# A mixture-of-experts layer on one core: the summing matmuls placed behind each block's gate/up matmuls, the down loads moved forward four blocks later, the halves of b_down side by side

## The reference: what is computed

```python
logits = hf @ w_router + b_router
top_v, top_e = lax.top_k(logits, TOP_K)          # 4 of 32
gates = jax.nn.softmax(top_v, axis=-1)
...
def expert_block(args):                          # for the tokens of one expert
    xblk, e = args
    gu = xblk @ w_gu[e] + b_gu[e]                # 1024 -> 2048
    gate = jnp.minimum(gu[:, :D_FF], SWIGLU_LIMIT)
    up = jnp.clip(gu[:, D_FF:], -SWIGLU_LIMIT, SWIGLU_LIMIT)
    act = (up + 1.0) * gate * jax.nn.sigmoid(SWIGLU_ALPHA * gate)
    return act @ w_dn[e] + b_dn[e]               # 1024 -> 1024
...
return h + moe                                   # sum over a token's experts, weighted by its gates
```

## Time and profile before

| | |
|---|---|
| time, median of 3 runs | 1166.12 us (1165.85 to 1166.32) |
| time of the profiled execution | 1166.64 us |
| its span in the profile | 1164.8 us, that is 1.84 us less |
| PE busy | 1106.0 us, 95% |
| DVE, ACT, POOL busy | 23%, 13%, 1% |
| moved by the DMA queues | 427.28 MB, mean 367 GB/s over the span |

### The profile page before, as it was taken

How to read it: one execution, slowest core, us unless ns; L and a number is a source line. 1 busy time by engine, 2 the same in 40 slices (tenths; PEclk the granted TensorE clock), 3 DMA queues, 4 the chain that set the end, 5 groups by cost and what they waited for, 6 DMA issues and landing times.

```text
span 1164.8 us, 13191 instructions
## 1 busy us (share of the span) xinstructions
PE 1106.0 (95%) x5236; PEld 446.8 (38%) x5236; DVE 269.5 (23%) x621; ACT 151.8 (13%) x285; POOL 8.0 (1%) x28
## 2 busy tenths in 40 slices
PE   9999989999999999989999999999999999999996
PEld 7855755533333333333333333333333333333332
DVE  3643344321111112121111111111111111111111
ACT  3521324400000000000000000000000000000000
POOL 1000000000000000000000000000000000000000
PEclk9999999999999999999999999999999999999999
DMA  9593110999999999999999987999999999999993
GB/s 326 97 383 119 73 73 5 397 416 428 426 429 428 429 429 427 432 430 388 419 432 431 430 362 291 433 429 430 431 430 431 431 430 431 431 430 430 432 428 145
DMA packets 36605, 427.28 MB, mean 367 GB/s; under 512 B 6083, under 2 KB 8228, under 8 KB 17380
## 3 DMA queue, kind: packets, MB, share of 16 engines
q1 hardware_dynamic: 34004, 426.33, 87.7%
q10 hardware_dynamic: 2576, 0.59, 0.2%
HBM read 424.29 MB, written 2.62 MB: 367 GB/s over the span
## 4 chain that ended last, share of the span: by engine, by line
PE 84%; DVE 7%; DMA 5%; issue 3%; ACT 1%; SPq 0%; DVEq 0%; ACTq 0%
PE bank L1629 36%; PE bank L1669 19%; PE bank L1569 5%; PE bank L1250 5%; DMA store<-in_w_down_dram 4%; PE bank L1257 4%; PE bank L1443 3%; PE bank L1617 3%; PE bank L1321 2%; DVE conv L1125 2%; DVE conv L1128 1%; DVE conv L1115 1%; PE bank L1655 1%; PE bank L1372 1%; DMA store<-in_w_in_dram 1%
## 5 line engine op out<-in xcount | busy, mean ns | idle before, releaser
L1629 PE MATMUL bank<-store,conv 128*64 128x512 f32 x2048 | 453.2, 597 | 0.0
L1629 PEld LDWEIGHTS bank<-store,conv 128*64 128x64 f32 x2048 | 142.8, 137 | 305.6 <-issue 304.0
L1669 PE MATMUL bank<-store,conv 128*64 128x512 f32 x1024 | 228.7, 599 | 9.9 <-DVE conv L1128 7.4
L1114 DVE TENSOR_SCALAR conv<-bank 128x512 f32<-128x512 f32 x32 | 22.1, 692 | 694.7 <-PE bank L1629 694.7
L1669 PEld LDWEIGHTS bank<-store,conv 128*64 128x64 f32 x1024 | 71.1, 138 | 144.9 <-issue 127.3
L748 ACT ACTIVATE conv<-conv 128x512 f32<-128x512 f32 x32 | 20.1, 629 | 542.9 <-DVE conv L1114 542.9
L1569 PE MATMUL bank<-qkT 64*128 64x512 f32 x256 | 63.6, 615 | 0.7 <-ACT qkT L755 0.7
L1372 PE MATMUL bank<-arena,qkT 128*64 128x512 f32 x256 | 62.2, 605 | 0.2 <-DVE qkT L927 0.2
L1250 PE MATMUL bank<-store 128*128 128x512 f32 x128 | 57.3, 600 | 0.0
L755 ACT COPY qkT<-bank 128x512 f32<-128x512 f32 x32 | 18.7, 585 | 281.1 <-PE bank L1669 281.1
L1655 PE MATMUL bank<-ident,conv 128*128 128x128 f32 x128 | 21.0, 287 | 24.3 <-DVE conv L1125 24.3
(11 more groups left out here) (284 smaller groups left out, 575.9 us busy)
## 6 DMA issues: line engine op xcount, KB each, us to landing
store<-in_w_gate_up_dram SPq DMA_DIRECT2D x42, 4096.0 KB, 23.5
store<-in_w_down_dram SPq DMA_DIRECT2D x64, 2048.0 KB, 13.8
store<-in_w_gate_up_dram SPq DMA_DIRECT2D x44, 2048.0 KB, 18.6
store<-in_w_in_dram SPq DMA_DIRECT2D x7, 2048.0 KB, 22.3
store<-in_w_out_dram SPq DMA_DIRECT2D x1, 4096.0 KB, 18.8
bias_by_distance<-store SPq DMA_DIRECT2D x1, 1536.0 KB
hx<-in_x_dram SPq DMA_DIRECT2D x2, 512.0 KB, 3.9
store<-bias_by_distance SPq DMA_DIRECT2D x1, 1024.0 KB, 8.3
```

The source lines that it names most:

```text
L1629: ins = mm(dst[SLOTS * hf:SLOTS * (hf + 1), :], xgT[:, c:c + SLOTS], store[:, slot_at(k, odd) + c0:slot_at(k, odd) + c0 + 512], start=Fals ...
L1669: ins = mm(bank[7][SLOTS * hf:SLOTS * (hf + 1), :], actT[:, c:c + SLOTS], w[:, hf * 512:(hf + 1) * 512], start=f == 0, stop=f == KT - 1)
```

## The change

1. `LATE_BLOCKS` goes from 16 to 20: the steps 16 to 19 of SP's loop now issue G(b+1) ahead of D(b), step 20 puts D between the halves, and D goes first from step 21 on (before: from step 17).
2. In the blocks from 10 on, other than the last, `combine()` moves from behind step k = 3 to behind the whole of gate/up, as it stands in blocks 1 to 9.
3. In `add_mixture` the two matmuls with `b_down` stand next to each other, and then the two with `ident`.

```diff
-LATE_BLOCKS = 16
+LATE_BLOCKS = 20
...
                     mm(bank[2 * t + hf][:], gT[t][rows, :], bdn[rows, :], start=False, stop=False,
                        skip_group_check=True)
+                for hf in range(2):
                     mm(bank[2 * t + hf][:], ident[:], hx[:, t, 512 * hf:512 * (hf + 1)], start=False, stop=False,
                        skip_group_check=True)
...
-                    if k == (5 if last else 3) and (whole or last):
+                    if k == 5 and last:
 
                         pe.wait_ge(y_ready, b)
                         combine()
-                        if last:
-                            turn_gates(b)
+                        turn_gates(b)
...
             def whole_block(b, odd):
                 gate_up(b, odd, whole=True)
+                pe.wait_ge(y_ready, b)
+                combine()
                 rest(b)
```

## The result

The changed kernel took 1150.44 us (median of 4 runs, 1148.77 to 1151.44) against 1166.22 us for the kernel before. The ratio is 0.9861, with a 95% interval of 0.9844 to 0.9879. Both lie within 1.2 us of the predicted 1149.5.

What follows compares the result with a forecast made beforehand. PE bounds the kernel before; after the change the loads do: G(30) lands at 1090.8, plus 20.6 to block 31, plus 36.7 gives span 1148.1, profiled 1149.9, predicted 1149.5 us; range 1146.5 to 1154.

Steps and rivals of the forecast that it cites:

- b_down: Between blocks 9 and 10: pairs on different rows and banks run side by side, saving 2.5 us in all.
- the rival: Ahead of G(12): b_down pairs save nothing, 2.0 to 3.4 us idle remain, time 1151.5 to 1153; chance 0.12.
- The turn: Where SP's order puts D ahead of G: queue idle 1.5 us before D(21), in place of 13.1 now.
- The early pockets: Queue idle 2.0 us at G(12)'s first half and 1.4 at its second; both taken as closed by earlier issue.
- Where PE waits: For down in blocks 18 and 19, some 1.5 us each; for gate/up in blocks 27 to 30, some 1.8 each.
- G(30)'s landing and block 31's start: End of the load chain: G(30)'s second half lands at 1090.8, block 31 starts 20.6 us later at 1111.4.
- The end: From block 31's start to the span's end: 36.7 us, taken as untouched by the change.
- What part 1 is worth: LATE_BLOCKS 20: about 4 us, as a turn at step 16 idles 5.1 to 5.6; nothing without part 2.
- PE remains the bound: Whole kernel: no waits for loads, block 31 starts at 1100.6, time 1139; chance 0.03.
- `combine`'s place isn't what PE waits for: Late blocks: the 1.18 us come from something else, only b_down counts, time 1164; chance 0.03.
- such a fall: Blocks 27 to 30: clock falls in PE's 1.8 us load waits, costing 2.7 us once; time 1152 or 1153; chance 0.13.
- The slower case: After the turn, every D(b) meets an empty queue, 3.0 us idle a block, time 1179; chance 0.03.

Runs made afterwards that it cites:

- bdown_only: Only the loop split in add_mixture that pairs the b_down matmuls, against the kernel before: 1163.62 us, ratio 0.9975.
- combine_late20: The full change without the add_mixture loop split (b_down as before): 1152.55 us, ratio 0.9877 to the kernel before.
- clock_fill: The full change plus seven unused 128x256 matmuls where the last block waits for the activation: 1147.64 us, ratio 0.9833 to the kernel before.
- late20_only: Only LATE_BLOCKS = 20, against the kernel before: 1166.14 us, ratio 0.9997.
- half_down: The full change, loading only half the down weights of blocks 9 to 29 (output not the layer's): 1138.85 us, ratio 0.9748 to the kernel before.
- combine_only: Only combine moved behind gate/up from block 10 on, against the kernel before: 1155.64 us, ratio 0.9909.
- last_behind: The full change plus combine and turn_gates behind gate/up in the last block too: 1145.90 us, ratio 0.9822 to the kernel before.
- the two padded kernels: The full change, and last_behind with two unused filling matmuls, each with 4.3 us PE time added between blocks 23 and 24: 1152.75 and 1146.90 us.

## Why the prediction was right

Its steps, against the profile:

- **A block on PE**: 27.5 us forecast, 27.51 measured; both waits on DVE gone.
- **b_down**: 2.5 forecast, 2.5 measured (8.4 to 5.9). Block 10's gate/up started at 520.8, 521.3 forecast. The alternative, that the pair would not run side by side, fell with bdown_only. What it would have cost, the pocket ahead of G(12), is seen in combine_late20, with 1152.55 us in the rival's 1151.5 to 1153.
- **The pace of the loads**: from D(10)'s landing at 533.0 to G(30)'s at 1090.8 it is 557.8 us, less 2.6 lost, over 19 blocks: 29.22 us, 29.26 forecast.
- **The turn**: 1.5 us idle forecast, 1.6 measured; D(21) was issued at 825.0 (824.6 forecast). What it cost before was read too low: ahead of D(16) the prediction counts 2.7 us, but the queue had been empty since G(17)'s first half landed at 692.6, so 3.4 were lost. All in all 17.2 us were lost before, not 15.9 or 16.5. Nothing in the sum hung on it.
- **The early pockets**: the first closed as forecast. The second didn't quite: G(12)'s second half came 0.65 us late and G(13)'s 0.4. In the repeat of the full change neither was late. The second was no pocket in the prediction's sense. Before, from 545.13 to 556.25, the queue had a DMA share of 0.97, and in combine_late20 G(12)'s second half was issued 5.5 us ahead of the first half's landing and still came 1.2 us late. So an earlier issue is not what closes it.
- **Where PE waits**: for down in blocks 18 and 19, forecast with 1.5 us each. Measured were 1.15 and 1.43 (0.27 + 1.16), and already 0.48 in block 17. In blocks 27 to 30 it waits 1.48 us each, 1.8 forecast.
- **G(30)'s landing and block 31's start**: 1090.8 and 1111.4 forecast, 1090.8 and 1111.45 measured. That exactness is luck: D(10) landed 0.4 us earlier than before, the pace took 0.7 less than reckoned, and the queue lost 1.1 more. In the repeat the two are 1089.65 and 1110.34. The weights of the last block were in time, as forecast, but the times given for them, 1110.5 and 1120.3, are those of G(31)'s two halves (1111.6 and 1121.4 measured); D(31) landed at 1131.2.
- **The end**: 36.7 us forecast from there, 38.25 measured. This term was mis-sized. I took it from the earlier trace rows as untouched; the clock falls in the wait of 3.28 us there, and it stayed low for 6.8 us where before it was 3.4. clock_fill shows that the low clock behind that wait is what these microseconds are: with the gap filled, down takes 7.09 us in place of 10.02. Two profiles of the same kernel end 38.25 and 36.7 us after block 31's start, so it varies from run to run; it is 1.5 of the 2.6 us by which these two spans differ.
- **What part 1 is worth**: about 4 us forecast. Block 31's start moved by 2.8 us against the first profile of the full change, and by 3.9 against the repeat, counted from D(10)'s landing; the times, 0.7 to 0.9 us apart, don't settle it. The step that was off is the idle time of a turn at step 16, 5.1 to 5.6 forecast, 4.2 measured: D(17) was issued at 711.0 as reckoned, but G(17) had landed at 709.5 in place of 709.0, and D(17) took 7.6 us, the lower of the two values. That it is worth nothing without part 2 is shown by late20_only.

Of the rivals, "PE remains the bound" has its time, 1139, in half_down, where the loads are fewer; with all loads it isn't so. That `combine`'s place isn't what PE waits for fell with combine_only, 11 us without `b_down`. The clock never fell in a waiting block: it is 1.00 from 828 to 1127, with waits of 1.48 us. The prediction had given such a fall 0.13. The slower case, a queue that goes empty ahead of every D(b), didn't come: one gap only, at the turn.

What the full change leaves is the loads' pace (11.6 us by half_down) and the last block's wait for the activation (4.7 us by last_behind).

## What to carry to other kernels

Where two resources are near their limits, work out both streams as clocks of their own, with the last landing that the rest hangs on, and take the later one; the time saved on the first counts only until the second takes over. Idle time of the slower stream costs one for one, wherever it lies, and nothing while the other is slower: the same shift of the turn moved the last block by nothing where PE was the slower, and by 2.8 us where the loads were. Ask then what triggers each load, since work on the faster engine still counts where it delays an issue, and look at the last round by itself, where a wait has no next round behind it to fill it.

## What the runs showed of the hardware that was not expected

- Second halves of gate/up land late, with the queue busy, only in company of a packet of kind "instruction". In the 13 profiles other than half_down there are 247 of them from G(12) to G(30). In 28 cases a 16 KB packet of that kind started between the first half's landing and their own: 19 of these landed 0.14 to 1.4 us late, 9 were on time. Without such a packet none of 219 was late. The late ones are G(12), G(13), and, in the two padded kernels alone, G(25). How late they are also goes with the issue of the next load: G(12)'s second half was 1.2 to 1.4 us late where D(11) was issued 4.8 to 6.4 us before it was due (five profiles), 0.25 to 0.85 at 6.3 to 6.9 (six), not late at 7.4, and in one exception, bdown_only, not late at 6.2. The issue alone doesn't do it: without the packet loads were on time with the next one issued as close. Neither cause was tried by a run of its own.
- Matmuls of 32 rows on two row groups, with 128 columns and different banks, run side by side: four passes in 1.06 us, where two took 1.05 when the shape changed after each pair. Four passes of 128 rows behind each other take 0.48 each (1.91 / 4), and two 0.53 each where the shape alternates.
- The clock stayed at full through idle gaps of 0.8 to 1.5 us in otherwise busy stretches. It fell in or just behind the gap of 2.3 to 2.4 us ahead of block 10, which follows small matmuls of 48 columns, and behind the one of 3.3 us in the last block. For this same gap the low clock lasted 3.4 us in seven profiles and 6.8 in three.
